# A decoder layer with a 128-tile expert sweep: a fourth ready-made u tile for each of seven heads, and zero writes and first scatters at later places

## The reference, cut to what matters

```
h = rms(x); q, k, v, B, C, xc = split(h @ w_in)           # 8 differential attention heads, 1024 conv channels
x = x + concat(attention(q, k, v), B * conv3(C * xc)) @ w_out
h2 = rms(x)
# PEER: 8 heads, 128 keys a half, 16 experts a token and head, out of 16384
experts, gates = top16(queries(h2) against the product keys)   # per token and PEER head
act = gelu(u[experts] . h2) * gates
x = x + sum over the 128 chosen experts of act * v[experts]
```

## Time and profile before

| | |
|---|---|
| median of 3 runs | 2944.31 us (2942.99 to 2944.36) |
| profiled execution, its own time | 2943.42 us |
| span of the profiled execution | 2941.6 us |
| PE busy | 2884.6 us, 98% of the span |
| DVE busy | 2374.1 us, 81% |
| POOL busy | 1589.7 us, 54% |
| ACT busy | 1054.5 us, 36% |
| DMA | 995.33 MB, mean 338 GB/s |

### The profile page before, as it was taken

How to read it: one execution, slowest core, us unless ns; L and a number is a source line. 1 busy time by engine, 2 the same in 40 slices (tenths; PEclk the granted TensorE clock), 3 DMA queues, 4 the chain that set the end, 5 groups by cost and what they waited for, 6 DMA issues and landing times.

```text
span 2941.6 us, 40454 instructions
## 1 busy us (share of the span) xinstructions
PE 2884.6 (98%) x14881; PEld 2557.2 (87%) x14881; DVE 2374.1 (81%) x3078; ACT 1054.5 (36%) x1375; POOL 1589.7 (54%) x1022
## 2 busy tenths in 40 slices
PE   8999999999999999999999999999999999999998
PEld 6888778878899999999999999999997888778777
DVE  6555788755679888988889898899777999889988
ACT  4121433341333333434333343344233333334333
POOL 1000444400115765666656566577867888877852
PEclk9999999999999999999999999999999999999999
DMA  8997887778868999999999899999999999999998
GB/s 296 332 356 271 284 275 262 248 283 312 302 235 311 325 349 316 333 326 341 319 323 340 301 338 330 335 338 368 330 360 395 408 419 416 418 420 420 421 417 359
DMA packets 327440, 995.33 MB, mean 338 GB/s; under 512 B 64565, under 2 KB 181313, under 8 KB 241793
## 3 DMA queue, kind: packets, MB, share of 16 engines
q1 hardware_dynamic: 179056, 515.94, 47.1%
q0 software_dynamic: 110656, 447.10, 42.1%
q10 hardware_dynamic: 37584, 30.43, 3.2%
HBM read 873.67 MB, written 119.67 MB: 338 GB/s over the span
## 4 chain that ended last, share of the span: by engine, by line
PE 69%; DVE 12%; DMA 7%; issue 5%; POOL 5%; ACT 1%; ACTq 0%; DVEq 0%; SPq 0%; POOLq 0%
PE ps L1979 21%; PE ps L1981 21%; PE ps L1980 21%; DMA v_ring<-in_peer_v,experts 4%; DVE x_rows L1829 3%; PE ps L2220 3%; POOL dots L946 3%; POOL v_ring L957 2%; DVE u_row L1820 2%; DMA v_two<-in_peer_v 1%; DVE uT_lo L1788 1%; DVE x_one L1927 1%; DVE uT_lo L1793 1%; DVE v_lo L1878 1%; DMA u_row<-in_peer_u,experts 1%
## 5 line engine op out<-in xcount | busy, mean ns | idle before, releaser
L1979 PE MATMUL ps<-hT_hi,uT_hi 128*128 128x384 f32 x2048 | 698.2, 341 | 8.1 <-DVE uT_lo L1788 4.6
L1981 PE MATMUL ps<-h2T_lo,uT_hi 128*128 128x384 f32 x2048 | 686.0, 335 | 0.0
L1980 PE MATMUL ps<-hT_hi,uT_lo 128*128 128x384 f32 x2048 | 684.9, 334 | 0.0
L938 POOL DMA_INDIRECT grid<-gates,grid_cells x256 | 518.6, 2026 | 105.3 <-issue 78.0
L1979 PE MATMUL ps<-v_hi,a_hi 128*128 128x512 f32 x1024 | 406.8, 397 | 23.5 <-DVE v_lo L1878 22.8
L1980 PE MATMUL ps<-v_hi,a_lo 128*128 128x512 f32 x1024 | 404.7, 395 | 0.0
L1981 PE MATMUL ps<-v_lo,a_hi 128*128 128x512 f32 x1024 | 404.6, 395 | 0.0
L1303 ACT ACTIVATE v_hi<-v_two 128x2048 fp32r<-128x2048 f32 x126 | 241.7, 1919 | 450.9 <-PE ps L1981 385.5
L1979 PEld LDWEIGHTS ps<-hT_hi,uT_hi 128*128 128x128 f32 x2048 | 384.7, 188 | 17.6 <-DVE uT_lo L1788 8.1
L1980 PEld LDWEIGHTS ps<-hT_hi,uT_lo 128*128 128x128 f32 x2048 | 385.0, 188 | 1.9
L1981 PEld LDWEIGHTS ps<-h2T_lo,uT_hi 128*128 128x128 f32 x2048 | 384.4, 188 | 0.0
(11 more groups left out here) (210 smaller groups left out, 4933.8 us busy)
## 6 DMA issues: line engine op xcount, KB each, us to landing
v_two<-in_peer_v SPq DMA_DIRECT2D x63, 2048.0 KB, 11.5
u_tile<-in_peer_u SPq DMA_DIRECT2D x65, 1024.0 KB
u_tile<-uT_all SPq DMA_DIRECT2D x63, 1024.0 KB
grid_rows<-grid SPq DMA_DIRECT2D x32, 1024.0 KB, 15.3
near_rows<-in_peer_u SPq DMA_DIRECT2D x25, 1024.0 KB, 8.7
uT_all<-near_turned SPq DMA_DIRECT2D x100, 256.0 KB, 7.0
w_raw<-in_w_in SPq DMA_DIRECT2D x24, 1024.0 KB, 9.1
wc_raw<-in_w_in SPq DMA_DIRECT2D x48, 512.0 KB, 6.0
```

The costliest lines, as they stand in the source:

```text
L938: pool.indirect_dma_start(out=grid, out_offset=bass.IndirectOffsetOnAxis(ap=grid_cells[:, d, col:col + 1], axis=0), in_=gates[:, 2 + d, co ...
L1979: mm(out, a_hi, b_hi, start=first, stop=False)
L1980: mm(out, a_lo, b_hi, start=False, stop=False)
L1981: return mm(out, a_hi, b_lo, start=False, stop=last)
```

## The change

- `EXTRA_AT` becomes (6, 14): tile 14 of PEER heads 0 to 6 is also turned before. 70 of 128 tiles come ready-made, and `kept_row` gives the seven new ones their rows of `uT_all`.
- Attention heads 0 to 6 have eight half turns instead of six: one at the start, one after `combined(0)`, two after `combined(1)` (one before), two after `combined(3)` (one before) and two after the normalised output (as before). `HALF_PLACES` says which buffer each uses: THIRD, LEFT, RIGHT, THIRD, LEFT, THIRD, RIGHT, LEFT. SP issues two more loads a head: 0 | 1, 2 | 3 | 4, 5 | 6, 7 at the five places instead of 0 | 1, 2 | 3 | 4 | 5. POOL issues eight more stores a head.
- The 16 zero writes: before, one in each attention head, four after the last output weights are ready and four after the keys are used. Now one in attention heads 1, 3, 5 and 7, one after the last head's output store, four and four at the two later places, and three in the sweep, in tile 1 of PEER head 0 behind its gathers.
- The scatters of PEER head 0 begin in tile 5 instead of tile 1: two there and three in each of tiles 6 to 15. The other heads' are unchanged.

```diff
-EXTRA = HEADS - 1
-EXTRA_AT = 6
-KEPT_BY_POOL = 1 + 3 * (HEADS - 1)
+EXTRA_AT = (6, 14)
+EXTRA = len(EXTRA_AT) * (HEADS - 1)
+KEPT_BY_POOL = 1 + 4 * (HEADS - 1)
...
+USES_A_HEAD = (3, 2, 3)
+HALF_PLACES = ((THIRD, 0), (LEFT, 0), (RIGHT, 0), (THIRD, 1), (LEFT, 1), (THIRD, 2), (RIGHT, 1), (LEFT, 2))
+TURNED_SINCE = (2, 1, 2, 2, 2, 1, 3, 2)
...
-    if tile % TOPK == EXTRA_AT:
-        return tile // TOPK < EXTRA
+    if tile % TOPK in EXTRA_AT:
+        return tile // TOPK < HEADS - 1
...
-                sp.wait_ge(seg_ready[NEAR], halves_turned(j, i) - 4)
+                sp.wait_ge(seg_ready[NEAR], halves_turned(j, i) - 2 * TURNED_SINCE[i])
...
-                    for i in ((), (0,), (1, 2), (3,), (4,), (5,))[p]:
+                    for i in ((), (0,), (1, 2), (3,), (4, 5), (6, 7))[p]:
...
             for j in range(HEADS):
-                zero_cells(j)
+                if j % 2 == 1:
+                    zero_cells(j // 2)
...
-                    for i in range(4):
+                    for i in range(6):
                         keep_half(j, i)
...
             store_o(HEADS - 1)
+            zero_cells(HEADS // 2)
             pool.wait_ge(w_ready, 4 * (QKV_CHUNKS + OUT_CHUNKS))
-            for n in range(HEADS, HEADS + 4):
+            for n in range(5, 9):
                 zero_cells(n)
             norm(1)
             pool.wait_ge(keys_used, 1)
-            for n in range(HEADS + 4, ZERO_DMAS):
+            for n in range(9, 13):
                 zero_cells(n)
...
-                    if b == 1:
+                    if (i, b) == (0, 1):
+                        for n in range(13, ZERO_DMAS):
+                            zero_cells(n)
+                    begin = 5 if i == 0 else 1
+                    if b == begin:
                         pool.wait_ge(gates_ready, 3 * i + 3)
                         pool.wait_ge(grid_done, 16 * (ZERO_DMAS + i * DENSE * TOPK))
                         pool.sem_inc(past_wait, 1)
-                    tiles = TOPK - 1 if i < PEER_HEADS - 1 else 11
+                    tiles = TOPK - begin if i < PEER_HEADS - 1 else 11
...
                 combined(1)
                 if not last:
                     turn_half_of_head(j, 2)
+                    turn_half_of_head(j, 3)
                 biased(3)
...
                 combined(3)
                 if not last:
-                    turn_half_of_head(j, 3)
+                    turn_half_of_head(j, 4)
+                    turn_half_of_head(j, 5)
                     split_wc(j + 1, 1)
```

40 lines of the change are left out of this document (22 added, 18 removed).

## The result

The changed kernel takes 2948.06 us (median of 20 runs, 2946.25 to 2952.38) against 2944.88 (20 runs, 2942.40 to 2949.69) measured beside it: **3.2 us or 0.12% slower**, ratio 1.0012 with a 95% interval of 1.0007 to 1.0018. That is under the 0.2% that I called what one can tell, and inside my range, but it is a real change and not the "no change" that I forecast. The profiled execution took 2947.81 us, its span is 2945.7.

What follows compares the result with a forecast made beforehand. PE was taken to set the pace, with DVE close behind in the sweep. 2943.42 - 5.4 + 5 + 0.3 = 2943.3 us for the profiled execution, 2944.3 for the median, no change that shows; range 2937.5 to 2951.5.

Steps and rivals of the forecast that it cites:

- term 1: Sweep, tile 14: transposes that go save PE 0.88 us a half; heads 1 to 5 gain 1.07 each, 5.4 us less.
- The 0 for head 6: Tile 14 of PEER head 6: DVE never rests there, so no gain was taken, at most 1.76 us.
- Rival D: Sweep: PE's transposes cost their full 272 ns durations, so seven tiles give 30.5 us, 2919; chance 0.01.
- term 2: PEER head 0: three more scatters in tiles 12 to 14 delay head 1's tile 0 gather; 5 us more.
- rival C: PEER head 0: every u gather from tile 7 waits behind one more scatter, 9.3 us, 2948.6; chance 0.22.
- term 3: Attention heads: two more half turns each, nearly hidden in DVE's idle time; 0.3 us more for all seven.
- the cover of DVE's turns: Attention heads: DVE's idle time, 2.19 us before `biased(3)` and 0.9 to 1.1 behind `combined(3)`, covers the added turns.
- hidden, if the loads come no later: Attention heads: 2 MB more DMA traffic a head, at a share of 0.79, costs nothing.
- rival B: Attention heads: the third buffer's half lands late before `biased(3)`, up to 1.5 us a head, 10.5 us, 2954.8; chance 0.10.

Runs made afterwards that it cites:

- e2: Kernel before with one edit: scatters of PEER head 0 begin in tile 5, three a tile from tile 6; 2952.31 us, ratio 1.0025.
- e3: Changed kernel with all zero writes and scatters at the places of the kernel before, so the fourth ready-made tile alone; 2945.53 us, ratio 1.0005.
- e10: Changed kernel with SP's load of half 5 moved behind the fifth weight piece; 2945.59 us, ratio 1.0002 to the kernel before.
- e4: Changed kernel with ACT's copy of the last transposed probabilities ahead of the next head's second weight split; 2946.36 us, ratio 1.0002 to the kernel before.
- e13: Kernel before with only its zero writes moved, seven of them ahead of the sweep; 2951.23 us, ratio 1.0021.
- e7: Changed kernel with old zero-write and scatter places, ACT's copy first in attention heads 0 to 6, fourth tile used in PEER heads 1 to 5 only; 2938.79 us.
- e11: Changed kernel with ACT's copy first in attention heads 0 to 6, head 0's scatters from tile 3, fourth tile used in PEER heads 1 to 5 only; 2940.00 us.
- e9: Fourth tile alone with ACT's copy first, plus three empty POOL semaphore instructions before each u gather of PEER head 0; 2945.58 us, ratio 1.0003 to kernel before.
- e1: Changed kernel with head 0's scatters from tile 1 and the three late zero writes ahead of the sweep; 2954.04 us, ratio 1.0028 to the kernel before.
- e12: e1 with ACT's copy ahead of the next head's weight split in attention heads 0 to 6; 2948.06 us, ratio 1.0012 to the kernel before.

## Why the prediction was right or wrong

- **Heads 1 to 5, term 1: right in mechanism, and nearly in size.** 1.07 us a head forecast, 1.09 in heads 1 and 3, but 0.3, 1.6 and 0.4 in heads 2, 4 and 5: 4.5 in all for 5.4 forecast. Head 2 lost 0.70 in a wait at 1421 us; head 5 lost 0.5 at the start of head 6, where the kernel before waited 1.51 and this one 2.04; head 4 gave 0.5 more because a wait of PE of 0.47 us at 1753.3 in the kernel before is gone. The 0 for head 6 was 0.5 in fact.
- **The rule of the Trainium skill against the rows: the rows decided.** 112 transposes are gone and PE's saving is 0.88 for eight of them (11.99 to 11.10, 9.22 to 8.35), as the distance of starts said, and not 8 x 0.27. Rival D is out.
- **Head 0, term 2: the sign right, the place wrong, the size too small.** "I take 5 us more" measured 6.5 in the changed kernel. The step that failed was to let POOL's slack absorb all lateness up to tile 11, to count only the three scatters of tiles 12 to 14, and so to expect that the gather of tile 0 of head 1 holds PE. That gather held nobody. (The prediction writes tile 1.0 for tile 0 of head 1.) PE lost its 5.54 us earlier, in tile 15, to the gather of tile 13, behind a row of tiles in which two gathers and three scatters fill POOL's time (10.6 us of 10.7); the signs were neither those of my forecast (4 us at the change to head 1) nor of rival C (four gaps of about 2), which e2 shows. Nor are the 6.5 all of the scatters: 2.9 are there in e3 with the scatters at their old places, and by the medians the changed kernel is 2.5 us above e3. The late scatters alone cost 7.2 by the median of e2.
- **Attention heads, term 3: wrong, and the largest part of the miss.** "I take 0.3 us for all seven" measured 3.5. My two steps were the cover of DVE's turns, which held (in head 0 the turn before `biased(3)` used 1.25 of its 2.19 idle us; where its half came 1.12, 0.63 and 0.26 us late, in heads 1, 3 and 5, PE still did not wait), and "on the DMA side ... hidden, if the loads come no later". I asked that of the half loads alone, and of rival B's third buffer alone. The transfer that came later was another one on the same queue, a weight piece (5.3 us to land for 3.8); I had priced the added loads by who waits for *them*, and not by who stands behind them in SP's queue. e10 and e4 each take it away.
- **Zero writes: costed at nothing.** The three in tile 1 cost nothing that the trace shows: tiles 0 to 7 of head 0 keep their distances to 0.04 us. The one behind the last output store may have part in the 0.9 of the output stage; no run has it alone. e13 shows 6 us where seven stand ahead of the sweep. I had not looked at why three are issued inside the sweep.
- **Sum.** 0.3 and 5 became 3.5 and 6.5 and the output stage 0.9 instead of nothing, heads 1 to 6 gave 5.0 instead of 5.4. With the measured terms, 2943.4 + 3.5 + 0.9 + 6.5 - 5.0 + 0.9 = 2950.2; the median is 2948.1, and the single executions' 1.9 in the dense stage is nearly all of the difference. The side to which it went was rival C's, nearly to its number (2948.6), by luck: it was not rival C's mechanism.

## What to carry to other kernels

A load that is added to a queue has to be priced three times: by who waits for it, by which older transfers it delays in the queue and on the DMA engines, and by what stands behind each of those waits in the order of the engine that waits. Before work on an in-order issuing engine is packed into fewer tiles, set its time for a tile against the tile's time: where nothing is left over, lateness that comes from elsewhere is not won back, and it shows at another place than the one where the work was added last. Where a saving is about the same in every repetition but its cost is not, take it only in the repetitions that have room: here heads 1 to 5 (e7 and e11, each 4.2 us below the same kernel with all seven). And where executions of one kernel spread by more than the effect, a stretch of one trace is not yet its price: compare it with the medians.

## What the hardware showed that I had not expected

**DVE holds POOL's issues for as long as it reads two SBUF operands.** Of the 256 scatters of the kernel before, those that start while DVE's dot, sum or a split from a loaded tile runs last as long as that instruction still has to go, plus 1.4 to 1.5 us (two that started 0.01 us into a dot did not); the shortest, and nearly all that start elsewhere, take 1.6. Two of the 77 in a dot: started 0.06 us into it, 3.71 us; 1.89 into it, 1.86. The 34 in a split `uT_lo<-u_tile,uT_hi` go from 2.66 (0.04 in) to 1.58 (1.10 in). But all 57 that start in a split `uT_lo<-ps,uT_hi`, the same operation on the same shape with one operand in PSUM, take 1.57 to 1.62, even 0.04 us behind its start. This is the rule of the Trainium skill, "SBUF — State Buffer", section "SBUF: two separate sides": DVE and GpSimd share a port pair that one of them holds for a whole instruction, and on DVE's side an instruction with two SBUF inputs takes it. The traces agree, and e9 shows it by experiment for one gather. No term of mine held it, though each tile that is turned beforehand moves two DVE splits from PSUM to SBUF. POOL's 256 scatters took 544.0 us in the changed kernel against 518.6; in the page of the changed kernel:

```profile
L950 POOL DMA_INDIRECT grid<-gates,grid_cells x256 | 544.0, 2125 | 78.0 <-issue 78.0
```

In the eleven kernels with the fourth tile they took 525.0 to 546.6, in the four without it 517.8 to 523.0. But the moved splits are not shown to be the reason: of the 25.4 us, 22.2 are in scatters that start in a dot (81 of them for 77, and earlier in it) and only 4.8 in those that start in a split from a loaded tile (35 for 34). In PEER head 0 the difference is 2.1 us (65.4 for 63.3), and what it costs the kernel was not measured.

**Hundredths of a us in a start can be worth 4 to 6 us**, by the chain of long issues that the traces of e1 and e13 have and that of e12 does not.
